# Eight gate tiles of each layer as split products whose low parts are made by adding DMAs

## The reference, cut to what matters

```
h = modulate(rms_norm_2(x, mixer_norm_g[l]), sh1, sc1)
proj = h @ w_in[l]                       # 1024 -> 2*512 + 512 + 2*1024
u_conv = proj[..., :2 * D_CONV]
u_pool = proj[..., 2 * D_CONV:2 * D_CONV + D_POOL]
gate_a, gate_b = split(sigmoid(proj[..., 2 * D_CONV + D_POOL:]), 2)
y_a = conformer_conv_branch(u_conv, ...) # a*sigmoid(g), 31 taps, layer norm, silu, matmul
y_b = pool_branch(u_pool, ...)           # window means 2,4,8,16, minus u, matmul
mixed = gate_a * y_a + gate_b * y_b
x = x + g1 * (mixed @ w_out[l])
h2 = modulate(rms_norm_2(x, ffn_norm_g[l]), sh2, sc2)
x = x + g2 * hierarchical_moe(h2, ...)   # 32 experts, 2 of them per token
```

## Time and profile before

| | |
|---|---|
| median of 3 runs | 1565.48 us (1562.48 to 1570.15) |
| the profiled execution | 1573.32 us, span 1571.6 us |
| PE / DVE / ACT / POOL busy | 92% / 58% / 37% / 0% |
| matmuls at L944 into `work` | 3 x 1024, 873 us in all |
| plain gate tiles (L979) | 512 records, 111.5 us |
| SP's queue | 414.19 MB on SP's queue |
| POOL's queue | 5.20 MB |

### The profile page before, as it was taken

One profiled execution on the slowest core, in us unless ns is written; L12 is line 12 of the kernel. 1 busy time (PEld: TensorE's weight loads), 2 busy tenths in 40 slices (PEclk: granted clock), 3 DMA queues, 4 the chain that ended last, 5 costly groups with the idle time before them and its releaser, 6 DMA issues.

```text
span 1571.6 us, 26923 instructions
## 1 busy us (share of the span) xinstructions
PE 1448.8 (92%) x10545; PEld 1172.6 (75%) x10560; DVE 905.9 (58%) x1607; ACT 577.5 (37%) x916; POOL 4.3 (0%) x10
## 2 busy tenths in 40 slices
PE   8999999989978899999999999987878999998876
PEld 7999999988977798999998989432215989642223
DVE  6898877684435466888886987410004997410002
ACT  4544346522344554434445143321104325321101
POOL 0000000000000000000000000000000000000000
PEclk9999999899989998999998999999988999999888
DMA  8999854412512345688883739899996848899996
GB/s 303 392 359 309 302 178 152 143 54 96 201 68 91 106 139 189 256 311 302 308 295 115 285 129 396 328 409 409 410 409 261 314 149 337 330 409 409 409 409 239
DMA packets 115851, 420.87 MB, mean 268 GB/s; under 512 B 12960, under 2 KB 13104, under 8 KB 115616
## 3 DMA queue, kind: packets, MB, share of 16 engines
q1 hardware_dynamic: 114624, 414.19, 70.7%
q0 software_dynamic: 1120, 5.20, 0.9%
HBM read 416.71 MB, written 2.62 MB: 267 GB/s over the span
## 4 chain that ended last, share of the span: by engine, by line
PE 69%; DMA 11%; SPq 6%; DVE 5%; ACT 4%; issue 3%; DVEq 0%; ACTq 0%
PE work L944 26%; PE acc L944 11%; PE work L979 7%; SPq L762 6%; PE work L1035 5%; DMA over_splits<-wstream_d 4%; PE work L1583 4%; PE work L904 2%; DMA c_act<-wstream_d 2%; DMA over_end<-wstream_d 2%; ACT whi L1673 1%; PE work L914 1%; DMA raw<-wstream_d 1%; DVE wlo L2127 1%; PE work L1610 1%
## 5 line engine op out<-in xcount | busy, mean ns | idle before, releaser
L2127 DVE TENSOR_TENSOR wlo<-raw,whi 128x1024 fp32r<-128x1024 f32 x264 | 320.7, 1222 | 171.5 <-ACT whi L1673 171.2
L1673 ACT ACTIVATE whi<-raw 128x1024 fp32r<-128x1024 f32 x264 | 276.9, 1056 | 274.4 <-PE work L944 186.2
L944 PE MATMUL work<-hhi,whi 128*128 128x256 f32 x1024 | 292.1, 285 | 3.1 <-DVE hlo L2155 1.5
L944 PE MATMUL work<-hhi,wlo 128*128 128x256 f32 x1024 | 290.4, 284 | 0.0
L944 PE MATMUL work<-hlo,whi 128*128 128x256 f32 x1024 | 290.3, 284 | 0.0
L944 PEld LDWEIGHTS work<-hhi,whi 128*128 128x128 f32 x1024 | 197.1, 192 | 6.0 <-DVE wlo L2127 2.8
L944 PEld LDWEIGHTS work<-hlo,whi 128*128 128x128 f32 x1024 | 197.0, 192 | 0.1
L944 PEld LDWEIGHTS work<-hhi,wlo 128*128 128x128 f32 x1024 | 196.8, 192 | 0.0
L2898 DVE TENSOR_TENSOR pair_b<-work,pair_a 128x256 f32<-128x256 f32 x16 | 6.8, 425 | 208.1 <-ACT pair_a L2080 208.1
L2238 DVE SCALAR_TENSOR_TENSOR ada_tiles<-ada_tiles,c_act 128x1024 f32<-128x1024 f32 x96 | 116.3, 1219 | 2.9 <-DMA ada_tiles<-ada_d 2.9
L979 PE MATMUL work<-hf,raw 128*128 128x256 f32 x512 | 111.5, 379 | 0.0
(11 more groups left out here) (499 smaller groups left out, 2701.5 us busy)
## 6 DMA issues: line engine op xcount, KB each, us to landing
raw<-wstream_d SPq DMA_DIRECT2D x364, 512.0 KB, 5.0
ada_tiles<-ada_d SPq DMA_DIRECT2D x96, 512.0 KB, 5.6
over_splits<-wstream_d SPq DMA_DIRECT2D x80, 512.0 KB, 15.2
over_select<-wstream_d SPq DMA_DIRECT2D x48, 512.0 KB, 14.3
tables<-wstream_d SPq DMA_DIRECT2D x34, 512.0 KB, 14.9
over_end<-wstream_d SPq DMA_DIRECT2D x24, 512.0 KB, 14.2
spare_d<-wstream_d SPq DMA_DIRECT2D x20, 512.0 KB, 14.0
over_pool<-wstream_d SPq DMA_DIRECT2D x20, 512.0 KB, 15.2
```

The lines of the kernel that those rows point to most:

```text
L944: mm = pe.matmul(out, a, b, start=(start and k == 0), stop=(stop and k == n - 1), skip_group_check=skip)
L1673: act.activation(whi[n % AHEAD][:], tiles[SLOT[SPLITS[n]]][:], ACT.Copy).then_inc(s("hi_done"), 1)
L2127: dve.tensor_tensor(wlo[n % AHEAD][:], tiles[SLOT[SPLITS[n]]][:], whi[n % AHEAD][:].bitcast(F32), ALU.subtract).then_inc(s("lo_done"), 1)
```

## The change

Every odd gate tile becomes a split tile, but its low part is made in another way. ACT writes the negated rounded tile into `wlo`, and then the high part into `whi` as ever. POOL then loads the same tile from HBM once more, into `wlo`, with a DMA that adds to what lies there, which leaves tile minus high part. When that has landed, POOL raises `lo_done` in place of DVE. DVE's next `lo` waits until POOL has done all eight.

The early expert loads are moved four tiles ahead (behind a4 to a7, p0 to p3 and G0 to G5). From G6 on SP issues the odd tile of each pair before the even one, and a buffer that held an odd gate tile is free when its high part is taken. Layer norm's sums come one tile later (the mean after G11, the router row and the variance after G12), in banks 1, 3 and 2 instead of 0, 2 and 1.

```diff
-        out += [(f"G{l}", m, False) for m in range(16)]
+        out += [(f"G{l}", m, m % 2 == 1) for m in range(16)]
...
-    out = {START[f"p{l}"] + j: [r] for j, r in enumerate(free)}
+    out = {START[f"a{l}"] + 4 + j: [r] for j, r in enumerate(free)}
...
+SOONER = {}
+for _l in range(LAYERS):
+    for _m in range(6, 16, 2):
+        SOONER.update({START[f"G{_l}"] + _m: START[f"G{_l}"] + _m + 1, START[f"G{_l}"] + _m + 1: START[f"G{_l}"] + _m})
...
-LN_MEAN_G, LN_VAR_G, SPLIT_G = 10, 11, 16 - AHEAD
+LN_MEAN_G, LN_VAR_G, SPLIT_G = 11, 12, 16 - AHEAD
...
+                elif q in SUMMED_NUMBER:
+                    sp.wait_ge(s("hi_done"), NUMBER[q] + 1)
...
-                    load(r)
+                    load(SOONER.get(r, r))
...
             for l in range(LAYERS):
+                for r in SUMMED[PER_LAYER * l:PER_LAYER * (l + 1)]:
+                    n, j = NUMBER[r], SUMMED_NUMBER[r]
+                    pool.wait_ge(s("negated"), after("negated", j + 1))
+                    pool.dma_start(wlo[n % AHEAD][:], wstream[r], accum_op=ALU.add).then_inc(s("rest_landed"), 16)
+                    pool.wait_ge(s("rest_landed"), after("rest_landed", 16 * (j + 1)))
+                    pool.wait_ge(s("hi_done"), n + 1)
+                    pool.wait_ge(s("lo_done"), n)
+                    pool.nop().then_inc(s("lo_done"), 1)
...
+            def hi_and_negated(r):
+
+                n = NUMBER[r]
+                tile_loaded(act, r)
+                act.wait_ge(s("pe_tile"), SPLITS[n - AHEAD] + 1)
+                act.activation(wlo[n % AHEAD][:], tiles[SLOT[r]][:], ACT.Copy, scale=-1.0).then_inc(s("negated"), 1)
+                hi(n)
+
...
                 for m in range(4):
+                    if m >= 2:
+                        hi_and_negated(START[f"G{l}"] + 2 * m - 3)
                     evac(START[f"p{l}"] + m, ppad[:, m, 16:16 + T], m % 4)
                 for m in range(16):
+                    if m == 0:
+                        hi_and_negated(START[f"G{l}"] + 5)
+                    elif m % 2 == 1 and m < 10:
+                        hi_and_negated(START[f"G{l}"] + m + 6)
                     evac(START[f"G{l}"] + m, gate2[:, m, :], m % 4, ACT.Sigmoid)
...
                 pooling(3).then_inc(s("pooled"), 1)
+                dve.wait_ge(s("lo_done"), NUMBER[START[f"pool{l}"]])
```

More of the change, by code:

```diff
@@ L345 @@
                             ("dn_z", LEVELS - 1), ("dn_vw", 2), ("dn_state", 1), ("dn_v1", 1),
-                            ("dn_osq", 1), ("dn_oroot", 1)]),
+                            ("dn_osq", 1), ("dn_oroot", 1), ("negated", LAYERS * 16)]),
+    **shared("rows_stored", [("rows_stored", 16), ("rest_landed", 16 * LAYERS * 16)]),
     **shared("cmp_products", [(n, 1) for n in ("parts_mm", "cmp_mm", "cmp_scores", "pct_mm", "cmp_values")]),
@@ L370 @@
     TAP_ORDER += [(c, sum(t[0] == c for t in TAP_ORDER)) for c in _left]
-LN_MEAN_G, LN_VAR_G, SPLIT_G = 10, 11, 16 - AHEAD
+LN_MEAN_G, LN_VAR_G, SPLIT_G = 11, 12, 16 - AHEAD
+SUMMED = [r for r in SPLITS if STREAM[r][0][0] == "G"]
+SUMMED_NUMBER = {r: n for n, r in enumerate(SUMMED)}
+PER_LAYER = len(SUMMED) // LAYERS
 NORM_PARTS = [1 if k in (8, 11) else 4 for k in range(8 + 3 * LAYERS)]
@@ L1459, in _ @@
                         pe.wait_ge(s("conv_done2"), l + 1)
-                        claim([0], "ln_centred", l + 1)
+                        claim([1], "ln_centred", l + 1)
                         for c in range(4):
-                            mm = pe.matmul(work[0][:, 0:T], ones, yconv[:, c, :], start=(c == 0), stop=(c == 3))
+                            mm = pe.matmul(work[1][:, 0:T], ones, yconv[:, c, :], start=(c == 0), stop=(c == 3))
                         mm.then_inc(s("ln_mean"), 1)
                     elif m == LN_VAR_G:
-                        claim([2], "router_row", l + 1)
+                        claim([3], "router_row", l + 1)
                         for c in range(DC):
@@ L1468, in _ @@
                             b = l * 48 + 3 * DC + c
-                            mm = pe.matmul(work[2][:, 0:36], spread(mod[:, b:b + 1], (P,), (0,)), params[:, a:a + 36],
+                            mm = pe.matmul(work[3][:, 0:36], spread(mod[:, b:b + 1], (P,), (0,)), params[:, a:a + 36],
                                            start=(c == 0), stop=(c == DC - 1))
                         mm.then_inc(s("router_row_mm"), 1)
-                        wide_part(k + 1, 1, 0, 4, ln_squares)
+                        wide_part(k + 1, 2, 0, 4, ln_squares)
                 pe.wait_ge(s("pooled"), l + 1)
@@ L2717, in _ @@
                 dve.wait_ge(s("ln_mean"), after("ln_mean", l + 1))
-                dve.scalar_tensor_tensor(yconv[:], spread(work[0][:, 0:1], (4, T), (0, 1)), -1.0 / 512, yconv[:],
+                dve.scalar_tensor_tensor(yconv[:], spread(work[1][:, 0:1], (4, T), (0, 1)), -1.0 / 512, yconv[:],
                                          ALU.mult, ALU.add).then_inc(s("ln_centred"), 1)
@@ L2722, in _ @@
                 dve.wait_ge(s("router_row_mm"), l + 1)
-                dve.tensor_tensor(router_row, work[2][:, 0:36], par(f"router_b{l}"), ALU.add).then_inc(s("router_row"), 1)
-                variance(k + 1, 512, src=work[1][:, 0:T])
+                dve.tensor_tensor(router_row, work[3][:, 0:36], par(f"router_b{l}"), ALU.add).then_inc(s("router_row"), 1)
+                variance(k + 1, 512, src=work[2][:, 0:T])
                 root_done(k + 1)
```

## The result

The changed kernel is slower. Its time was 1578.66 us (median of 5, 1575.73 to 1581.78) against 1569.29 us for the kernel before on the same chips; the ratio is 1.0054, with a 95% interval of 1.0034 to 1.0075, about 8.5 us. It was run again later beside other kernels: 1.0040 (1.0018 to 1.0062).

What follows compares the result with a forecast made beforehand. PE was taken to bound the gate stage, DMA the expert stages. Saving 2 x (4.6 - 0.3) = 8.6 us from the 1565.48 us median gave 1556.9, predicted as 1557; range 1554 to 1578 us.

Steps and rivals of the forecast that it cites:

- rival C: Expert stages: being DMA bound, they do not pass on the gate stage's shift; time stays 1565 us; chance 0.07.
- price of the tiles: Gate stage on PE: plain tile 3.45 us, split 2.88; eight odd tiles save 4.6 us a layer, 9.2 for both.
- ACT's added work: Odd gate tiles: two ACT passes of 1056 ns each, 17 us a layer, fit into ACT's idle time.
- the moved loads: Fourteen early loads four places ahead, odd loads earlier: cost nothing, or one landing, 5 us, if a5 came late.
- layer norm's later sums: Gate stage: sums one tile later wait for nothing; pool tile in time by 0.3 us, a thin cover.
- well ahead: Gate stage: raw tiles for ACT's negated copies are there early, G1's load issued at 864.60, others a tile apart.
- D: Cycle of POOL's serial adding DMAs: wait for negation, issue, landing, tell PE; taken as 5.6 us.
- the prediction's own sum: Gate stage: PE loses 6D - 39.3 us a layer by G11, nothing up to D = 6.55.
- rival A: Gate stage: adding DMA too slow once D passes 6.55 us; at D = 8.2, 1576 us; chance 0.24.
- crowd: Early loads issued 856 to 877 us, DMA engines full: first adding DMAs about 8 us, G1 costs 0.3 us.
- nothing is to be had or lost: Gate stage: PE's clock was granted in full, so it was to bring no gain and no loss.
- Rival E: Tap stretch: busy DVE keeps POOL from writing descriptors; 39 us of stall a layer, 1634 us; chance 0.03.

Runs made afterwards that it cites:

- yardstick: The changed kernel as it is, run again on the chip of the later runs, against the kernel before: ratio 1.0040.

## Why the prediction was wrong

The bound was read rightly. PE was the chain of the gate stage, and a change of that stage is passed on in full through the DMA bound expert stages: the table shows it, and rival C is out. The price of the tiles was right: plain tiles stayed at 3.45 us and split ones at 2.87, and with nothing late the stage is shorter by 4.66 us in the chain against 4.6 forecast.

ACT's added work, the moved loads and layer norm's later sums cost nothing, as said. The raw tiles were not all "well ahead", though: in the changed trace ACT waited 2.1 us for G7's and 1.3 us for G11's before their negated copies, which ended at 888.0 and 910.2, still ahead of POOL's issues at 900.78 and 917.33. G1's adding DMA was issued at 876.97, where the prediction had 876.2 with PE's p tiles 0.6 us earlier. In the changed trace nothing waits between the sums and the pool tile (chain above, from 926.21), and the output tiles begin 14.1 us behind the pool tile's start, 14.2 before.

The step that failed is the adding DMA: "I take the row whose traffic is likest [...] D = 5.6". D was 7.7 us on average over the six cycles from G1's issue to G13's (46.4 us), and 7.9 us in layer 1. Put into the prediction's own sum, 6 x 7.7 - 39.3 = 6.9 us, and 8.0 in layer 1; measured, the stages are 63.07 - 55.95 = 7.1 and 8.3 us longer than with nothing late. (PE's last wait was at G9 and not at G11; the same sum for five cycles gives 40.4 - 33.0 = 7.4 us.) So the sum was right and its input wrong, and rival A, with its threshold of 6.55, came true: the forecast had it at 0.24. Had I taken 7.7, the forecast would have been 1565.5 + 2 x (6.9 - 4.6) = 1570 us, against the 1565.5 for before, and the measured ratio says 8.5 us more than before where that says 4.6. The measured 1578.66 lies 0.7 us above the range; beside it the kernel before measured 1569.29, and not the 1565.48 from which the range was drawn.

How was D wrong? Hardly for a DMA by itself: with no collision the cycle is 5.7 to 6.4 us. Its landing was right too. The source reads of the Trainium skill (Collectives: The Full Stack, section The bandwidth ceiling: the fold count and why AG ≠ RS ≠ AR) had given an estimated 5.4 us where landings without collision mostly took 5.1 to 5.5; the part of it that was for the adding, 1.3 us, is twice the 0.7 us or so between these and the plain loads' 4.5 to 4.8. The 0.2 us for two semaphore hops, which no row gave, were 0.6 us. But a margin of 1 us to the threshold was taken for safety although the prediction had noted two raw loads at each pair's end, and collisions made cycles of 8.2 to 8.3 us. D was also treated as a constant with chance around it. It depends on when the pair is issued, and that depends on PE: once PE waits for a landing, it does a split and a plain tile, 6.3 us, and SP's next pair goes out just as POOL issues the DMA after the next. One late landing makes the next late. The first was late because its DMA had only 7.6 us between the negated copy and PE's need, and took 9.2 to 10.0; the prediction saw about 8 there and priced it at 0.3 us, once, without asking what a late PE does to the rest. Why the first takes 8.6 us even with two in flight and no crowd stays open.

That "nothing is to be had or lost" by PE's clock held in the changed kernel's first trace. The waits put it at risk: in the yardstick the clock fell behind all three of them.

Rival E, POOL's descriptors kept back by DVE, did not happen: they were written in 0.83 to 0.90 us while DVE ran the taps, as the rule of the Trainium skill (SBUF — State Buffer, section Who interferes with whom) has it for DVE instructions with two SBUF operands.

## What to carry to other kernels

A serial chain of DMAs that feeds PE at nearly its own pace needs a head start and not only a rate: with the crowd away, 2.9 us sooner took 13.6 us off the two gate stages, a second DMA in flight 10.8. Ask of each such chain what is issued into the same DMA engines just ahead of each of its members, and whether a wait of the consumer moves those issues onto them. Where a threshold lies within 1 us of a duration that no trace shows, both sides of it deserve much the same chance.

## What the runs showed of the hardware

- A DMA of a 512 KB tile that adds to what lies in SBUF, from POOL's queue: landing mostly 5.1 to 5.5 us undisturbed, 9.2 to 10.5 us beside the crowd; the same without adding 4.5 to 4.8 and 5.7 to 6.4. POOL was at each issue for 0.85 us, against 0.53.
- Two raw loads of 512 KB issued from 1.7 us ahead to 0.3 us behind such a DMA came with landings 1.5 to 3 us longer in most cases; issued 1 to 4 us behind it, with none but for one case (landing 7.8 us, the pair 1.0 us behind). Plain loads by POOL with a pair issued that near took 3.6 to 5.7 us (three cases).
- Two adding DMAs, to different tiles, can be in flight at once: landings then had a median of 7.1 to 7.5 us, with one started every 5.1 to 5.6 us on average.
- After idle times of 2.0 to 3.1 us at PE the granted clock could fall to its lower level of 1.2 GHz: in the yardstick, behind the 2.51 us ahead of G1 in layer 1, the granted clock was 0.50 in the window of 1254 to 1256 us and the split tile took 4.4 us and not 3.0. Behind 2.47 us in the changed kernel's first trace it stayed at 1.00. So a wait of 2.5 us may cost 4. Columns as in the earlier trace rows:

```profile
1252.00:1254.00 2.00, 1.36 (x7) 1.36 (x8) 2.00 (x7) 1.04 (x2) 0.82 (x1) 0.72 0.92 340
1254.00:1256.00 2.00, 2.00 (x11) 2.00 (x11) 1.97 (x6) 0.97 (x2) 0.03 (x1) 0.50 0.93 244
1256.00:1258.00 2.00, 2.00 (x15) 1.89 (x14) 2.00 (x6) 0.38 (x1) 0.00 (x0) 0.92 0.89 174
```
